# Dilated attention's scores with the two 64-feature halves alternating, and the norm between the two blocks placed later

## The reference, cut to what matters

```python
sc = jnp.einsum('bchnqd,bchnkd->bchnqk', qs, ks).astype(jnp.float32) + bias[:, None]
sc = jnp.where(mask, sc, NEG_INF)
lse = jax.nn.logsumexp(sc, axis=-1)
pr = jnp.exp(sc - lse[..., None]).astype(vs.dtype)
o = jnp.einsum('bchnqk,bchnkd->bchnqd', pr, vs)
...
wts = jax.nn.softmax(jnp.stack(lses, axis=0), axis=0).astype(q.dtype)
o = jnp.sum(wts[..., None] * jnp.stack(outs, axis=0), axis=0)
```

```python
    return rmsnorm(x, final_norm_g)
...
        x = x + 0.5 * swiglu(rms_norm(x, norm_ffn1[l]), ffn1_w1[l], ffn1_w3[l], ffn1_w2[l])
```

## Time and profile before

| | |
|---|---|
| median of 3 runs | 2107.19 us (2106.38 to 2108.09) |
| profiled execution, its own time | 2108.3 us |
| its span, first to last instruction | 2106.5 us |
| TensorE busy | 2066.2 us, 98% of the span |
| VectorE, ScalarE, GpSimd busy | 1176.6, 866.3, 329.3 us |
| mean granted TensorE clock | 0.994 of full |

### The profile page before, as it was taken

One profiled execution on the slowest core, in us unless ns is written; L12 is line 12 of the kernel. 1 busy time (PEld: TensorE's weight loads), 2 busy tenths in 40 slices (PEclk: granted clock), 3 DMA queues, 4 the chain that ended last, 5 costly groups with the idle time before them and its releaser, 6 DMA issues.

```text
span 2106.5 us, 26969 instructions
## 1 busy us (share of the span) xinstructions
PE 2066.2 (98%) x10562; PEld 1742.4 (83%) x10562; DVE 1176.6 (56%) x2216; ACT 866.3 (41%) x1644; POOL 329.3 (16%) x526
## 2 busy tenths in 40 slices
PE   8999999999999999999999999999999999999998
PEld 7777898888888888878888889978898888888887
DVE  6676556666444344575443446675875664443445
ACT  6455434444423233453332224555554443332225
POOL 2311000021000000131110102431451011110101
PEclk9999999999999999999999999999999999999999
DMA  5141332213332232223333323213243123333223
GB/s 168 61 132 58 105 100 72 72 61 100 111 97 89 95 100 100 84 77 100 100 100 100 99 81 106 76 61 110 91 140 100 41 81 100 100 100 100 94 78 129
DMA packets 197879, 198.62 MB, mean 94 GB/s; under 512 B 3820, under 2 KB 193068, under 8 KB 197676
## 3 DMA queue, kind: packets, MB, share of 16 engines
q1 hardware_dynamic: 197752, 196.89, 29.5%
HBM read 194.66 MB, written 6.93 MB: 96 GB/s over the span
## 4 chain that ended last, share of the span: by engine, by line
PE 88%; DVE 4%; issue 3%; POOL 2%; ACT 2%; DMA 0%; SPq 0%; DVEq 0%; POOLq 0%; ACTq 0%
PE ps L600 24%; PE ps L606 24%; PE ps L603 24%; PE ps L609 2%; PE ps L612 2%; PE ps L615 2%; DVE m L640 1%; POOL m L692 1%; PE ps L1101 1%; PE ps L1390 1%; PE ps L1859 1%; PE ps L1381 0%; POOL m L1678 0%; DVE m L1126 0%; PE ps L709 0%
## 5 line engine op out<-in xcount | busy, mean ns | idle before, releaser
L600 PE MATMUL ps<-m,m 128*128 128x512 f32 (+1 forms) x2432 | 950.4, 391 | 1.5 <-ACT m L889 1.5
L606 PE MATMUL ps<-m,m 128*128 128x512 f32 (+1 forms) x2432 | 939.3, 386 | 0.0
L603 PE MATMUL ps<-m,m 128*128 128x512 f32 (+1 forms) x2432 | 938.6, 386 | 0.5 <-DVE m L640 0.5
L631 ACT ACTIVATE m<-m 128x512 fp32r<-128x512 f32 x688 | 399.8, 622 | 572.9 <-PE ps L606 544.2
L640 DVE TENSOR_TENSOR m<-m,m 128x512 fp32r<-128x512 f32 x688 | 515.2, 766 | 67.5 <-ACT m L631 64.0
L606 PEld LDWEIGHTS ps<-m,m 128*128 128x128 f32 x2432 | 457.6, 188 | 93.7 <-DVE m L911 0.6
L600 PEld LDWEIGHTS ps<-m,m 128*128 128x128 f32 x2432 | 458.1, 188 | 92.2 <-issue 3.4
L603 PEld LDWEIGHTS ps<-m,m 128*128 128x128 f32 x2432 | 458.3, 188 | 87.6 <-DVE m L640 0.7
L1595 POOL TENSOR_TENSOR m<-m,m 128x512 f32<-128x512 f32 x44 | 76.2, 1732 | 493.1 <-DVE m L1572 493.1
L609 PE MATMUL ps<-m,m 128*128 128x256 f32 x512 | 149.7, 292 | 0.0
L612 PE MATMUL ps<-m,m 128*128 128x256 f32 x512 | 146.2, 286 | 1.5 <-DVE m L640 1.4
(11 more groups left out here) (329 smaller groups left out, 1953.4 us busy)
## 6 DMA issues: line engine op xcount, KB each, us to landing
m<-ffn_w SPq DMA_DIRECT2D x60, 1024.0 KB, 5.3
m<-w_ff SPq DMA_DIRECT2D x32, 1024.0 KB, 5.4
m<-w_in SPq DMA_DIRECT2D x28, 1024.0 KB, 5.2
m<-ffn_w SPq DMA_DIRECT2D x12, 768.0 KB, 4.5
m<-w_in SPq DMA_DIRECT2D x17, 512.0 KB, 5.1
m<-w_out SPq DMA_DIRECT2D x8, 1024.0 KB, 5.2
m<-mem_w_kv SPq DMA_DIRECT2D x8, 1024.0 KB, 5.4
m<-w_out_a SPq DMA_DIRECT2D x4, 1024.0 KB, 5.2
```

Of the source, the lines that this page charges most:

```text
L600: pe.matmul(o, lh, xh, start=k == 0, stop=False)
L603: pe.matmul(o, ll, xh, start=False, stop=False)
L606: done = pe.matmul(o, lh, xl, start=False, stop=k == nk - 1)
L631: act.activation(self.WH[b % 2][:, at], self.RAW[b % 2][:, at], ACT.Copy).then_inc(*self.up("w_hi", b, c))
```

## The change

It has two parts.

The scores of the two halves `m` of one (`pair`, `r`) are issued together: each product of `m` = 0 is followed by the same product of `m` = 1. So `pe_attend_b` handles a pair of units, 8 times instead of 16. Half `m` now has two banks of its own for scores and for turned probabilities both: 2 and 3 for `m` = 0, 4 and 5 for `m` = 1. The places are in line with this: a pair of units every 1.0 block (0.94 in the second pair of heads) instead of a unit every 0.5 (0.47), the transposes 0.5 and 0.63 block behind the scores.

`both_place` puts the norm of both blocks at 1.05 blocks behind the start of `ff1`, where it stood at 0.65; the first silu stands at 1.85 instead of 1.25, `dve_x_normed` from 4.6 instead of 1.4.

```diff
         for h in range(4):
-            yield (self.start["qkb0"] + 0.1 if h < 2 else self.place_b(0, 3, h - 2) + 0.5)
+            yield (self.start["qkb0"] + 0.1 if h < 2 else self.place_b(0, 3) + 0.13 * h + 0.25)
...
-    def place_b(self, pair, r, m):
+    def place_b(self, pair, r):
         if pair == 0:
-            return self.start["vb0"] + 1.2 + 0.5 * (2 * r + m)
-        return max(self.start["vb1"] + 0.25, self.place_b(0, 3, 1) + 0.6) + 0.47 * (2 * r + m)
+            return self.start["vb0"] + 1.2 + r
+        return max(self.start["vb1"] + 0.25, self.place_b(0, 3) + 1.1) + 0.94 * r
 
     def place_weigh_b(self, pair, r, m):
-        return self.place_b(pair, r, m) + (1.05 if pair == 0 else 1.1)
-
-    def pe_attend_b(self, pe, new, pair, r, m):
-        n, half, q = 2 * r + m, slice(64 * m, 64 * m + 64), slice(r * P, (r + 1) * P)
-        u, s = 8 * pair + n, self.place_b(pair, r, m)
+        return self.place_b(pair, r) + (1.05 if pair == 0 else 1.0) + 0.12 * m
+
+    def pe_attend_b(self, pe, new, pair, r):
+
+        q, s = slice(r * P, (r + 1) * P), self.place_b(pair, r)
         hi, lo = self.QKB[pair]
         yield s
-        for w in new(self.at("qkb_lo", 6 * pair + 5), *self.claim(("qk_b", pair, n), 2, 3)):
+        units = [(m, 2 * r + m, slice(64 * m, 64 * m + 64)) for m in range(2)]
+        claims = [w for m, n, half in units for w in self.claim(("qk_b", pair, n), 2 + 2 * m, 3 + 2 * m)]
+        for w in new(self.at("qkb_lo", 6 * pair + 5), *claims):
             pe.wait_ge(*w)
-        out = self.bank(("qk_b", pair, n))
         for g, (c0, c1, k) in enumerate(((0, 512, slice(0, S)), (512, 640, q), (640, 768, q))):
-            pe.matmul(out[:, c0:c1], hi[half, g, q], hi[half, 3 + g, k], start=True, stop=False)
-            pe.matmul(out[:, c0:c1], hi[half, g, q], lo[half, 3 + g, k], start=False, stop=False)
-            done = pe.matmul(out[:, c0:c1], lo[half, g, q], hi[half, 3 + g, k], start=False, stop=True)
-        done.then_inc(*self.full(("qk_b", pair, n)))
-        yield s + 0.48
-        for w in new(self.at("probs", "b", u), *self.claim(("turn_b", pair, n), 4, 5)):
-            pe.wait_ge(*w)
-        out = self.bank(("turn_b", pair, n))
...
+            for step, (x, y) in enumerate(((hi, hi), (hi, lo), (lo, hi))):
+                for m, n, half in units:
+                    done = pe.matmul(self.bank(("qk_b", pair, n))[:, c0:c1], x[half, g, q], y[half, 3 + g, k], start=step == 0, stop=step == 2)
+                    if g == 2 and step == 2:
+                        done.then_inc(*self.full(("qk_b", pair, n)))
+        for m, n, half in units:
+            yield s + 0.5 + 0.13 * m
+            for w in new(self.at("probs", "b", 8 * pair + n), *self.claim(("turn_b", pair, n), 2 + 2 * m, 3 + 2 * m)):
+                pe.wait_ge(*w)
+            out = self.bank(("turn_b", pair, n))
+            for c in range(6):
+                done = pe.transpose(out[:, c * P:(c + 1) * P], self.PB[m][:, c * P:(c + 1) * P], self.ident)
...
+        for m, n, half in units:
+            yield self.place_weigh_b(pair, r, m)
...
+            for w in new(self.cleared(("turn_b", pair, n)), *values, *self.claim(name, 6 + m)):
+                pe.wait_ge(*w)
...
     def dve_attend_b(self, dve, new, pair, r, m):
-        n, s = 2 * r + m, self.place_b(pair, r, m)
+        n, s = 2 * r + m, self.place_b(pair, r) + 0.13 * m
...
     def act_attend_b(self, act, new, pair, r, m):
-        n, s = 2 * r + m, self.place_b(pair, r, m)
+        n, s = 2 * r + m, self.place_b(pair, r) + 0.13 * m
...
     def silu_place(self, name, t):
-        return max(self.up_place(name, 0, t, 2) + 0.05, self.start[name, "up", 0] + (1.25 if name == "ff1" else 1.0) + 0.25 * t)
+        return max(self.up_place(name, 0, t, 2) + 0.05, self.start[name, "up", 0] + (1.85 if name == "ff1" else 1.0) + 0.25 * t)
...
+    def both_place(self):
+        return self.start["ff1", "up", 0] + 1.05
...
-        s += [self.pe_norm_both(pe, new, b["ff1", "up", 0] + 0.65)]
+        s += [self.pe_norm_both(pe, new, self.both_place())]
...
-        s += [self.pe_attend_b(pe, new, pair, r, m) for pair in range(2) for r in range(4) for m in range(2)]
+        s += [self.pe_attend_b(pe, new, pair, r) for pair in range(2) for r in range(4)]
...
-        s += [self.act_norm_both(act, new, b["ff1", "up", 0] + 0.65 + 3.5 * US)]
+        s += [self.act_norm_both(act, new, self.both_place() + 3.5 * US)]
...
-        s += [self.dve_norm_both(dve, new, b["ff1", "up", 0] + 0.65 + 0.8 * US), self.dve_x_normed(dve, new, b["ff1", "up", 0] + 1.4)]
+        s += [self.dve_norm_both(dve, new, self.both_place() + 0.8 * US), self.dve_x_normed(dve, new, b["ff1", "up", 0] + 4.6)]
```

More of the change, by code:

```diff
@@ L1405, in pe_attend_b @@
-        done.then_inc(*self.full(name))
+            for step, (x, y) in enumerate(((hi, hi), (hi, lo), (lo, hi))):
[10 more added lines that the diff above has]
+                done = pe.transpose(out[:, c * P:(c + 1) * P], self.PB[m][:, c * P:(c + 1) * P], self.ident)
+            done.then_inc(*self.full(("turn_b", pair, n)))
@@ new lines, in pe_attend_b @@
+        for m, n, half in units:
+            yield self.place_weigh_b(pair, r, m)
+            name, (th, tl) = ("pv_b", pair, n), self.PTB[m]
+            values = [self.cleared(("vb", pair, 0)), self.cleared(("vb", pair, 2))]
+            values += [self.cleared(("vb3", 0)), self.cleared(("vb3", 2))] if pair == 0 else [self.at("kept_lo", 3)]
+            for w in new(self.cleared(("turn_b", pair, n)), *values, *self.claim(name, 6 + m)):
+                pe.wait_ge(*w)
+            out = self.bank(name)[0:64, 0:P]
+            for c in range(6):
+                g, rk = (0, c) if c < 4 else (c - 3, r)
+                vh, vl = (y[:, rk, g, 64 * m:64 * m + 64] for y in self.VB)
+                pe.matmul(out, vh, th[:, c * P:(c + 1) * P], start=c == 0, stop=False)
+                pe.matmul(out, vh, tl[:, c * P:(c + 1) * P], start=False, stop=False)
+                done = pe.matmul(out, vl, th[:, c * P:(c + 1) * P], start=False, stop=c == 5)
+            done.then_inc(*self.full(name))
```

## The result

The changed kernel takes 2088.14 us (median, 2087.63 to 2088.37), the kernel before 2107.02 beside it (2106.38 to 2108.09): ratio 0.991, 95% interval 0.9892 to 0.9927, 0.9% less time. The forecast was 2085.5 with a range of 2083.3 to 2090.3. The profiled execution took 2087.63 us, 20.7 less than the profiled one of before; the sum had said 21.7.

A forecast was written before the change was run, and what follows sets the result against it. TensorE, busy 98% of the span, was taken as the bound. Scores 13.7, less 0.1 waiting, plus norm 8.1 make 21.7 us: 2108.3 becomes 2086.6, and 1.1 lower for the median, 2085.5; range 2083.3 to 2090.3.

The forecast's parts named there:

- the sum: Whole kernel: scores and norm together save 13.7 - 0.1 + 8.1 = 21.7 us, giving 2086.6 from the profiled 2108.3.
- A visit costs 1.71: Scores: 18 alternating products cost what nine did, 1.71 us; eight visits take 13.7 us instead of 27.4.
- the ring of banks: Scores, second class of second pair: TensorE waits 0.1 us for the second half's banks, shared by scores and transposes.
- rival b: Scores: pairs overlap only in part, 2090.8, or not at all, 2096; chance 0.08, 0.02 of it without any overlap.
- the prediction's estimate: Scores: at 77% of ideal packing a visit costs 2.2 us, and the total gain is about 4 us smaller.
- The norm gains 8.1: Norm of both blocks: its price on TensorE falls from 11.1 to 3.0 us with the later place and full clock.
- low rows: Norm: TensorE waits 0.3 us for ScalarE's low rows, after 19 wide products behind the one-column products.
- rival (a): Norm: the clock falls to half all the same, for some 9.6 us, losing 4.4: 2089.9; chance 0.12.
- The granted clock is full in every slice: Whole kernel, from the profile page: TensorE's clock is never reduced, so the time is TensorE's program, busy 98%.
- The moved silu and normed values are free: Around the norm: the later silu and `dve_x_normed` cost nothing, as banks and x's new value are needed much later.
- (c): Scores: L1433 late by 2.3 us at six visits, a new wait at shared banks, together 4.2 us: 2089.7; chance 0.10.
- (d): Scores: VectorE so late at the shared banks that TensorE's clock drops, about 11 us a stop; three stops 2119; chance 0.02.

The follow-up runs named there:

- the repeated execution: The changed kernel, unchanged, run again on one chip beside three variants of the norm's place: 2087.51 us, ratio 0.9905.
- eight groups: Changed kernel with the norm at 1.12 blocks, its one-column products in eight groups of two, row products seven steps later: 2085.60 us, ratio 0.9896.
- the kernel with the scores alone: Changed kernel with the norm, silu and normed values back at their old places, new scores kept: 2094.19 us, ratio 0.9934 to the kernel before.

## Why the prediction was right, point by point

- **A visit costs 1.71.** Right: 1.70, and 0.15 more in the one visit with a wait. The 0.1 us foreseen for the ring of banks there was 0.15. Scores: 13.3 us measured, 13.7 - 0.1 predicted; with the visits after at 8 x 1.70 + 0.15, before's sixteen units must have come to 27.1, not 27.4. What was not seen is that only 7.8 of them need the alternation; the way between full and half rows was estimated at 0.4 a visit (rival b) and is 0.3.
- **Rival b, no overlap: 2096.** With both heads in one half it is 2100.5: the saved ways are 2.4 us, not 3.2, and some 3 us go to a half clock that the rival did not have. The Trainium skill, "TensorE: Matmul & The Clock Gate", section "Measured speedup vs the span model", has 3.07 times for four products on quarters of the rows, and the prediction's estimate took 77% from that. For halves this loss is not seen: 18 products took 1.70 us, nine 1.71.
- **The norm gains 8.1.** This is the step that was mis-sized. Its terms were right at full clock: wait 0.7 (0.69), one-column products 1.95 (1.8 and 0.1 for the way out), low rows 0.3 (0.2 idle, but 0.4 by the distances of starts, with the way into and out of the stop); price 3.0, measured 3.2 (11.1 less the gain of 7.9) in the repeated execution. In the profiled one rival (a) came true in small: the clock fell, the low rows' wait vanished behind it (1.6 lost at half clock, 0.4 saved), and the price was 4.3, gain 6.8. The rival's price of 4.4 was four times too high, since it let the half clock last 9.6 us, and it lasts 3.4 here.
- **The granted clock is full in every slice.** This reading of the earlier trace rows says too much: a digit of 9 is 90% or more of a slice of 53 us, and the 10.2 us at half clock at the norm hide in one. The windows of the earlier trace rows, which the sum goes by, have them.
- **The moved silu and normed values are free.** Right: no wait on them, even with the rows 5 us later (eight groups).
- **No new wait at the shared banks, (c) and (d).** Right, but for the 0.15.
- **Own time and median.** Before's profiled execution lay 1.1 us above its median and after's 0.5 below its own. The sum, set against before's own time, gives 2086.6 against 2087.63; the forecast of the median took off 1.1 that after's median did not have. Of the 2.6 us between 2085.5 and 2088.1 this makes 1.6 (1.1 and 0.5), the norm 1.3 and the scores 0.3; the 0.5 from behind the norm goes the other way.

## What to carry to other kernels

Products that use half the rows should stand next to products of the other half: two fifths of what that brought here (5.5 of 13.3 us) came from putting them in one visit at all, the rest from alternating them. A step that waits for another engine should stand as late in TensorE's program as its reader allows: eighteen products of other work took the place of 4 us of wait and of up to 10 us at half clock, and three more took the last 0.7. With differences of one or two us, compare stretches of the traces between equal instructions; the whole times hide them.

## What the runs showed of the chip

- The products of different halves of the rows don't only overlap: a product of one half starts ahead of narrow ones of the other half that stand before it in the program, by 0.33 us at 335.64. That each engine runs its program strictly in order, as the section on the kernel before has it, does not hold for these starts.
- The clock can fall with TensorE never idle: 0.50 from 305 to 308 and again from 411 to 414 us in one kernel, from 341 to 343 and from 412 to 415 in the other, behind visits whose 18 products all used rows 0 to 63. What it answers to is open.
- The same instructions of the norm had half clock behind them in four executions and full clock in three, for 1.1 us; the kernel after itself showed both.
- The start of the program differs from execution to execution: the scores began at 300.88 to 303.42 us with equal instructions ahead of them. One reason is how long the clock is at half near 30 us. From 28 to 42 us the granted clock is 0.76 in five executions, where the scores began at 300.88 to 301.81, and 0.63 in the other seven, where they began at 302.49 to 303.42. The earliest start is that of the kernel with the scores alone; from 30 to 40 us its clock is 0.66 where the earlier trace rows has 0.50:

```profile
30.00:40.00 10.00, 10.00 (x60) 10.00 (x60) 8.99 (x32) 3.07 (x11) 0.00 (x0) 0.66 0.08 11
```
